# Half of the low weight halves beside two convolutions moved from VectorE to GpSimd, with the first convolution's steps set closer

## What is computed

```python
def first_block(x, ...):
    proj = rms_norm(x, pre_mix_g) @ w_in
    a, gate, q, k, v = split(proj)
    u = a * sigmoid(gate)                       # 256 x 1024
    u = depthwise_conv(u, w_dw) + b_dw          # 31 taps along the sequence, the "first convolution"
    yc = silu(layer_norm(u))
    ya = neighbourhood_attention(q, k, v, rpb)
    x = x + rms_norm(concat(yc, ya) @ w_out)    # the "first norm": this one and the pre-norm of the MLP
    f = square(relu(rms_norm(x) @ w_up)) @ w_down
    return x + rms_norm(f)                      # the "second norm", with the pre-norm of the next block

def second_block(x, ...):
    proj = rms_norm(x) @ w_in_2
    qk = silu(causal_depthwise_conv(concat(q_a, k_a)))   # 4 taps, the "second convolution"
    y_a = mlstm_chunkwise(...) ; y_b = causal_attention(...)
    return x + (sigmoid(g_a) * y_a @ w_a + sigmoid(g_b) * y_b @ w_b) @ w_out_2
```

## Time and profile before

| what | value |
|---|---|
| three runs | 2149.02, 2149.03, 2149.6 us; median 2149.03 |
| the profiled execution | 2148.05 us, of it 2146.2 us span (first to last instruction) |
| TensorE busy | 2133.0 us, 99% of the span |
| VectorE busy | 1408.7 us, 66% |
| ScalarE busy | 1088.7 us, 51% |
| GpSimd busy | 60.6 us, 3% |
| granted TensorE clock | 1.00 of full speed over the whole span |

### The profile page before, as it was taken

The page is one execution under the profiler, slowest core; times in us unless marked ns, Lnnn a source line. Parts: engine busy times, 40 slices in busy tenths (PEclk is TensorE's granted clock), DMA queues, the critical chain, the costliest instruction groups (busy, mean ns, idle before and its releaser), DMA issues.

```text
span 2146.2 us, 27253 instructions
## 1 busy us (share of the span) xinstructions
PE 2133.0 (99%) x9724; PEld 1763.6 (82%) x9724; DVE 1408.7 (66%) x1914; ACT 1088.7 (51%) x1515; POOL 60.6 (3%) x70
## 2 busy tenths in 40 slices
PE   9999999999999999999999999999999999999999
PEld 7888887888888888888877888888888888888887
DVE  6898857765655656656667646666445766766764
ACT  6545565654444444444475544554444655564452
POOL 1000100000000000000000000000000010000000
PEclk9999999999999999999999999999999999999999
DMA  9565446676776766767566765656666665656985
GB/s 329 186 188 163 150 146 215 205 217 196 238 201 208 212 202 204 212 191 216 175 199 212 239 189 172 202 193 200 204 203 200 201 192 156 189 175 193 334 269 165
DMA packets 187749, 436.68 MB, mean 203 GB/s; under 512 B 83032, under 2 KB 83552, under 8 KB 187360
## 3 DMA queue, kind: packets, MB, share of 16 engines
q1 hardware_dynamic: 185584, 429.03, 64.2%
q0 software_dynamic: 1744, 5.77, 0.9%
q10 hardware_dynamic: 288, 0.14, 0.0%
HBM read 407.60 MB, written 10.49 MB: 195 GB/s over the span
## 4 chain that ended last, share of the span: by engine, by line
PE 92%; DVE 4%; ACT 1%; issue 1%; SPq 1%; DMA 1%; POOL 0%; ACTq 0%; DVEq 0%
PE g L629 29%; PE g L631 29%; PE g L630 29%; DVE wlo L1474 1%; PE s L608 1%; SPq L2348 1%; DVE arena L1845 1%; DMA raw<-in_w_in 1%; PE s L686 1%; PE s L819 0%; PE s L818 0%; ACT whi L908 0%; DVE arena L1549 0%; DVE ta_lo L1661 0%; PE s L668 0%
## 5 line engine op out<-in xcount | busy, mean ns | idle before, releaser
L1474 DVE TENSOR_TENSOR wlo<-raw,whi 128x1024 fp32r<-128x1024 f32 x732 | 888.5, 1221 | 531.5 <-ACT whi L908 527.0
L908 ACT ACTIVATE whi<-raw 128x1024 fp32r<-128x1024 f32 x732 | 768.9, 1057 | 658.1 <-PE g L631 601.0
L629 PE MATMUL g<-whi,ta_hi 128*128 128x512 f32 x1920 | 761.5, 397 | 5.1 <-DVE wlo L1474 1.4
L631 PE MATMUL g<-whi,ta_lo 128*128 128x512 f32 x1920 | 748.9, 390 | 0.0
L630 PE MATMUL g<-wlo,ta_hi 128*128 128x512 f32 x1920 | 747.9, 390 | 0.0
L629 PEld LDWEIGHTS g<-whi,ta_hi 128*128 128x128 f32 x1920 | 361.0, 188 | 83.0 <-issue 6.7
L631 PEld LDWEIGHTS g<-whi,ta_lo 128*128 128x128 f32 x1920 | 360.7, 188 | 76.8
L630 PEld LDWEIGHTS g<-wlo,ta_hi 128*128 128x128 f32 x1920 | 361.3, 188 | 72.5
L629 PE MATMUL g<-whi,tb_hi 128*128 128x512 f32 x1008 | 396.6, 393 | 0.2 <-ACT arena L1097 0.2
L631 PE MATMUL g<-whi,tb_lo 128*128 128x512 f32 x1008 | 392.7, 390 | 0.0
L630 PE MATMUL g<-wlo,tb_hi 128*128 128x512 f32 x1008 | 392.3, 389 | 0.0
(11 more groups left out here) (236 smaller groups left out, 997.4 us busy)
## 6 DMA issues: line engine op xcount, KB each, us to landing
raw<-in_w_in SPq DMA_DIRECT2D x318, 512.0 KB, 3.9
raw<-in_w_up SPq DMA_DIRECT2D x128, 512.0 KB, 3.8
raw<-in_w_down SPq DMA_DIRECT2D x128, 512.0 KB, 4.2
raw<-in_w_out SPq DMA_DIRECT2D x64, 512.0 KB, 4.2
raw<-in_w_a SPq DMA_DIRECT2D x32, 512.0 KB, 4.2
raw<-in_w_b SPq DMA_DIRECT2D x32, 512.0 KB, 6.4
raw<-in_w_ukv SPq DMA_DIRECT2D x16, 512.0 KB, 4.3
raw<-in_w_uq SPq DMA_DIRECT2D x12, 512.0 KB, 3.8
```

Source lines behind the costliest of these rows:

```text
L629: e.matmul(o, xh, wh, start=first, stop=False)
L631: ins = e.matmul(o, xl, wh, start=False, stop=last)
L908: e.activation(whi[u % RING][:, 0:n], raw[u % RAW][:, 0:n], ACT.Copy).then_inc(s_hi, 1)
L1474: e.tensor_tensor(l, r, h.bitcast(F32), ALU.subtract).then_inc(s_lo, 1)
```

## The change

- A list `BY_POOL` of 49 units is made: every second one from 20 to 76 (29 units, of the stripes gate1 to v1, beside the first convolution), 116, 118 and 120 (behind the first norm), and every second one from 372 to 404 (17 units; the first three stand behind the second norm, the rest beside the second convolution).
- The low halves of these are made by GpSimd (a new `low` in `pool`), with the same subtraction on the same operands. It counts them on a semaphore of its own, and every GpSimd instruction that writes waits for the one before to be complete (`last_done`), as before. VectorE leaves them out.
- `low_at` says which semaphore and value the matmuls and the loads wait for.
- Steps of the first convolution are placed at `E("a0") + 9 + 5 * k // 11`: 2.2 a slot instead of 2.

```diff
+        BY_POOL = [v for a, b in ((by["a0"].last + 5, by["v1"].first + 6), (by["up00"].first + 4, by["up00"].first + 9),
+                                  (by["qk20"].first + 4, by["va0"].first + 4)) for v in range(a, b, 2)]
+
+        def low_at(u, j=1):
+
+            before = len([v for v in BY_POOL if v <= u])
+            return (p_lo, before) if u in BY_POOL else (s_lo, split_at(u, j) - before)
...
+        p_lo = Later(km_zero, 4)
...
                 if j == 0 or u < 2:
                     q.wait_ge(s_hi, split_at(u, j))
-                    q.wait_ge(s_lo, split_at(u, j))
+                    q.wait_ge(*low_at(u, j))
...
-                            yield max(E(f"a{n}") + 9, E("a0") + 9 + k // 2)
+                            yield max(E(f"a{n}") + 9, E("a0") + 9 + 5 * k // 11)
...
                 for u in units:
-                    if u >= 2:
+                    if u >= 2 and u not in BY_POOL:
                         low(u)
...
+            def low(u):
+                r, h, l = raw[u % RAW][:, 0:size(u)], whi[u % RING][:, 0:size(u)], wlo[u % RING][:, 0:size(u)]
+                q.wait_ge(s_hi, split_at(u))
+                q.wait_ge(s_mm, u - RING + 1)
+                last_done()
+                alone(e.tensor_tensor(l, r, h.bitcast(F32), ALU.subtract), p_lo.sem, 4 + BY_POOL.index(u) + 1)
...
-            for slot in range(total_slots):
+            for slot, units in slots_and_splits():
                 for g in sides:
                     g.upto(slot)
+                for u in units:
+                    if u in BY_POOL:
+                        low(u)
...
                 if u >= RAW:
                     q.wait_ge(s_hi, split_at(u - RAW))
-                    q.wait_ge(s_lo, split_at(u - RAW))
+                    q.wait_ge(*low_at(u - RAW))
```

## The result

The changed kernel takes 2185.66 us (median of five runs, 2183.09 to 2186.06); the kernel before takes 2149.03 us (2148.43 to 2149.6). The ratio is 1.0172, with a 95% interval of 1.0161 to 1.0182: slower by 36.6 us, where 14 us were forecast. It lies outside the forecast's range.

A forecast was written before the change was run, and what follows sets the result against it. TensorE's own pace, busy 99%, plus few waits was taken as the bound. Terms 12.1 - 2.0 + 2.0 + 1.7 = +13.8 us on the 2149.0 median gave 2162.8, rounded to 2163 us; range 2144 to 2170.

The forecast's parts named there:

- 2.0 taken: Every GpSimd low half: its subtraction holds VectorE off for 2.0 us, chosen between bounds of 0 and 3.4.
- part (3): First convolution: VectorE overloaded by 1.18 us per two units, 19.5 us less the lead, +12.1; then layer norm -2.0.
- the lead of 7.4: First convolution: VectorE's low half ends 7.4 us before TensorE needs it; overload costs nothing until it reaches that.
- The closer steps' 5.2 us of cost: First convolution: of the 12.1 us wait, 0.32 us a pair of units, 5.2 us, comes from closer steps.
- The layer norm's -2.0: Layer norm: TensorE arrives with the convolution's steps done, so its 2.0 us wait goes.
- The norms' +1.0 each: Two norms: a low half delays residual steps, about 1.5 us reaching TensorE, less a 0.50 wait: +1.0 each, +2.0 both.
- The second convolution's +1.7: Beside the second convolution: two chain low halves on GpSimd each remove 1.14 us and hold VectorE 2.0, +1.7 in all.
- The loads' zero: Loads waiting for GpSimd's low half are issued at most about 1 us later, hidden by the lead: no cost.
- The rival of the longer hold: Rival: GpSimd holds VectorE longer than 2.0 us; at 2.4 us, about 2170 us; no separate chance given.

The follow-up runs named there:

- writing only: Changed kernel with GpSimd filling the 49 low halves with zeros, reading nothing, in place of the subtraction: 2141.39 us, ratio 0.9964.
- the repeated low halves: Kernel before with five low halves in the MLP repeated 7 to 12 times by VectorE, without GpSimd: 2173.96 us, ratio 1.0118.
- the MLP run: Kernel before with GpSimd making every second low half of 29 units in the MLP's middle, none elsewhere: 2148.38 us, ratio 0.9998.

## Why the prediction was wrong

**The mechanism was right.** GpSimd's reading holds VectorE off (writing only: 2141.39 us), one subtraction by 2.16 us (2.0 taken), and VectorE is busy throughout from 100 to 157 us. The size was wrong by 23 us; of part (3), +12.1 less 2.0, 23.2 were measured.

**The step that failed** is the end of (3): "From 157 on VectorE had 17 us idle in 100, and the steps run out sooner; I add nothing." By its place in the weight stream TensorE is 11.8 us late at unit 55 (174.5 us against 162.7), and 23.8 at unit 88, behind the layer norm. So up to about 157 us the forecast's 12.1 came out near, and behind it, where nothing was added and 2.0 taken off, another 12 us came. TensorE is idle for 11.4 us from 157 to 257 us, though VectorE is busy only 91% of that time.

The lead behind it fails too, in "Less the lead of 7.4, TensorE waits 12.1 us there". The lead was read from one low half (the matmul that it is for starts at 101.60, so it is 7.1) and used as that of all of VectorE's work. Overload makes every piece in the queue late, and the ones with less lead are waited for first: the GLU, whose lead was 5.2 us, and from 157 us on the pieces that go on through ScalarE, which wait although VectorE has idle time on average. With half as many subtractions the low halves' waits are gone and these remain, 4.6 of the 6.3 us. How much of the 12 us is backlog carried over from before 157 us, and how much the holds behind it, no run separates. That the 12.1 came out near is in part luck: of what makes it up only 3.3 us are waits for low halves, 5.2 are the GLU's, and 2.3 are the clock, which the forecast did not have.

**A term was missing**: the halved clock, 10 of the 35 us. Beside the first convolution it is 6.9 us (half of 4.58, 3.41 and 5.80). The profile before holds no wait over 2.0 us, so it could not be read there; its 1.00 in every window was taken for a constant.

**The rest by its steps.** The closer steps' 5.2 us of cost: 5.4 by unit 76, but lost again at the layer norm, so that the old distance is as slow in the end (2184.64); alone they change nothing (2148.98). The layer norm's -2.0: right that this wait goes, but with the steps alone other waits took its place. The norms' +1.0 each: +7.6 for both; VectorE's residual steps meet a subtraction in several places, not one, and 1.7 of it is the clock (3.4 us at half). The second convolution's +1.7: +3.4, the wait of 1.41 us became 3.53 and brought 3.4 us of halved clock, of which 1.7 is the cost; without the clock the term was about right. The loads' zero: ScalarE's high halves do wait for them, 3.6 and 3.8 us before 95.13 and 102.08 us, in the changed kernel; whether that cost TensorE anything of its own was not tried. The rival of the longer hold (2170 us) has the wrong reason: the hold was not longer, its consequences were.

## What to carry to other kernels

Before moving work to GpSimd, ask what it reads: an instruction with two SBUF inputs took 2.16 us from VectorE for the 1.14 us it saved, so here the move lost in each of the three places where VectorE or a chain through it had no slack, and brought nothing where it had. When an engine gets overloaded, list every kind of piece in its queue with its lead and take the shortest, those that go on through another engine first; the average busy share says nothing of them. And price a long wait of TensorE with the halved clock behind it, here 1.6 to 2.9 us more for each wait of 2.44 to 5.16 us.

## What the runs showed of the hardware

TensorE's granted clock went to half (1.2 of 2.4 GHz) at or behind all five waits of 2.44 us and more in the changed kernel, and behind the three of 3.09 us and more in the MLP, for stretches of 3.4, 6.8 and once 10.2 us. It stayed full behind the MLP's waits of 1.41 and 1.77. But the length of the wait does not settle it. The kernel with GpSimd's low halves at the old distance has both exceptions: half behind a wait of 1.43 us, and full behind one of 2.45 (also behind one of 3.51, for another 5.0 us). Rows and windows of it (start or window, then as above):

```profile
396.78 0.85 PE L735 MATMUL s<-cst,arena 128*128 128x128 f32 x4 [1.43 <-DVE arena L1665]
...
397.20:400.40 3.20, 3.20 (x10) 2.49 (x9) 3.17 (x10) 2.49 (x9) 0.00 (x0) 0.50 0.54 163
...
411.77 0.66 PE L735 MATMUL s<-cst,arena 128*128 128x128 f32 x4 [2.45 <-DVE arena L1665]
...
409.00:420.00 11.00, 8.55 (x41) 6.89 (x40) 8.64 (x15) 7.27 (x17) 3.35 (x2) 1.00 0.57 195
```

At the layer norm's wait of 2.0 us it went both ways: 1.00 in the kernel before, in that with the subtractions behind the norms only and in that with the repeated low halves, but 0.50 in four others, two of them with no change near it. Window of the kernel with 29 low halves in the MLP, behind its wait of 1.99 us at 259 us:

```profile
260.40:263.70 3.30, 3.30 (x12) 0.50 0.53 159
```

So a kernel with a wait of that length can vary by some 1.7 us from run to run, which may be part of the spread of the kernel before (2146.45 to 2152.57 us in 27 runs). The Trainium skill ("TensorE: Matmul & The Clock Gate", section "Part 1: The HAM clock gate") has the low clock as the idle state, which activity releases; the rows agree, and add that it returns in the midst of a kernel whose TensorE is 98% busy.

A second surprise is how the hold on VectorE's convolution steps goes by what GpSimd does: none for a write of 128 x 1024 (longest step 0.62 us), 0.78 to 0.88 us for a copy of one input, 2.16 for the subtraction of two. It is not only two-input instructions of VectorE that are held. A copy of 128 x 1024 int16 values, one input, takes 0.69 us alone and 2.78 beside a subtraction in the MLP run. A multiply of 128 x 256 by a scalar (L1853), 0.35 us alone, takes 1.13 beside one of the pure writes.
